# New latents divided by tokens (128, then 192), with the query-latent tiles evicted between the parts

## The reference, cut to what matters

```python
h = rmsnorm(x, lp['norm_mix'])
proj = h @ lp['w_in']                       # pool, q_b, k_b, v_b, q_lat, kv_lat, kr_raw, gates
c_kv = rmsnorm(kv_lat, lp['mla_kv_norm'])   # 256 latents for each of the 320 new tokens
k_rope = apply_rope(kr_raw, pos)
lat_all = jnp.concatenate([past[0], c_kv], axis=1)          # 512 cached tokens come first
kv = (lat_all @ w_kvup).reshape(B, K, MLA_HEADS, MLA_NOPE_DIM + MLA_V_DIM)
k = rmsnorm(jnp.concatenate([k_nope, kr], axis=-1), qk_k_norm)
```

## Time and profile before

| what | value |
|---|---|
| median of 3 runs | 1046.33 us (1045.97 to 1047.3) |
| profiled execution | 1047.23 us |
| its span (first to last instruction) | 1045.3 us |
| granted TensorE clock, mean | 0.998 of full speed |
| PE busy | 1038.8 us (99%) |
| DVE busy | 641.6 us (61%) |
| ACT busy | 506.8 us (48%) |
| POOL busy | 314.3 us (30%) |

### The profile page before, as it was taken

How to read it: one execution, slowest core, us unless ns; L and a number is a source line. 1 busy time by engine, 2 the same in 40 slices (tenths; PEclk the granted TensorE clock), 3 DMA queues, 4 the chain that set the end, 5 groups by cost and what they waited for, 6 DMA issues and landing times.

```text
span 1045.3 us, 20059 instructions
## 1 busy us (share of the span) xinstructions
PE 1038.8 (99%) x7586; PEld 1005.6 (96%) x7586; DVE 641.6 (61%) x1079; ACT 506.8 (48%) x930; POOL 314.3 (30%) x277
## 2 busy tenths in 40 slices
PE   8999999999999999999999999999999999999998
PEld 6899999999999999999998999999999999999998
DVE  6888764445766666543567886554557565565443
ACT  6557755444554444434355585554445444433341
POOL 3365566541221111100133755656312211111000
PEclk9999999999999999999999999999999999999999
DMA  7455533244535544454514544333344354444441
GB/s 243 118 157 124 185 103 120 90 133 142 161 120 164 159 146 155 142 180 145 178 45 137 149 145 135 96 119 122 120 154 152 124 177 141 154 147 146 156 145 67
DMA packets 48707, 146.29 MB, mean 140 GB/s; under 512 B 8800, under 2 KB 14400, under 8 KB 48640
## 3 DMA queue, kind: packets, MB, share of 16 engines
q1 hardware_dynamic: 42416, 143.05, 44.3%
q10 hardware_dynamic: 6224, 2.30, 0.9%
HBM read 142.11 MB, written 3.22 MB: 139 GB/s over the span
## 4 chain that ended last, share of the span: by engine, by line
PE 97%; DVE 2%; DMA 0%; ACT 0%; issue 0%; SPq 0%; ACTq 0%
PE psum L566 29%; PE psum L567 28%; PE psum L568 28%; PE psum L739 1%; PE psum L778 1%; PE psum L761 1%; PE psum L721 1%; PE psum L722 1%; PE psum L726 1%; PE psum L769 1%; PE psum L698 1%; PE psum L811 1%; PE psum L994 0%; PE psum L866 0%; PE psum L693 0%; PE psum L694 0%
## 5 line engine op out<-in xcount | busy, mean ns | idle before, releaser
L566 PE MATMUL psum<-AH,WH 128*128 128x320 f32 x1328 | 414.4, 312 | 0.2
L568 PE MATMUL psum<-AH,WL 128*128 128x320 f32 x1328 | 410.3, 309 | 0.0
L567 PE MATMUL psum<-AL,WH 128*128 128x320 f32 x1328 | 410.2, 309 | 0.0
L566 PEld LDWEIGHTS psum<-AH,WH 128*128 128x128 f32 x1328 | 249.3, 188 | 7.3 <-issue 5.5
L567 PEld LDWEIGHTS psum<-AL,WH 128*128 128x128 f32 x1328 | 249.4, 188 | 0.2
L568 PEld LDWEIGHTS psum<-AH,WL 128*128 128x128 f32 x1328 | 249.3, 188 | 0.0
L1077 ACT CAST WH<-raw 128x1024 fp32r<-128x1024 f32 x166 | 172.7, 1046 | 129.2 <-PE psum L568 127.7
L1515 DVE TENSOR_TENSOR WL<-raw,WH 128x1024 fp32r<-128x1024 f32 x103 | 127.6, 1240 | 114.0 <-ACT WH L1077 113.6
L1978 POOL TENSOR_TENSOR WL<-raw,WH 128x1024 fp32r<-128x1024 f32 x60 | 147.6, 2478 | 114.7 <-ACT WH L1077 95.5
L1709 DVE TENSOR_TENSOR WL<-raw,WH 128x1024 fp32r<-128x1024 f32 x88 | 107.5, 1222 | 49.5 <-ACT WH L1250 48.2
L1983 POOL TENSOR_TENSOR fab<-fa,fb 128x320 f32<-128x320 f32 x44 | 38.6, 878 | 264.6 <-DVE fb L1714 264.6
(11 more groups left out here) (284 smaller groups left out, 1580.1 us busy)
## 6 DMA issues: line engine op xcount, KB each, us to landing
raw<-w_all SPq DMA_DIRECT2D x264, 512.0 KB, 3.5
y_out<-X SPq DMA_DIRECT2D x8, 160.0 KB, 2.7
X<-x_in SPq DMA_DIRECT2D x2, 320.0 KB, 5.7
X<-x_in SPq DMA_DIRECT2D x1, 640.0 KB, 7.4
lat_out<-ckv ACTq DMA_DIRECT2D x2, 320.0 KB, 2.9
scratch<-brel SPq DMA_DIRECT2D x8, 63.8 KB, 4.3
ckv<-lat_in SPq DMA_DIRECT2D x1, 384.0 KB, 5.5
bias<-scratch SPq DMA_DIRECT2D x8, 48.0 KB, 4.5
```

The source lines that it names most:

```text
L566: mm(out, WH[:, slot, c0:c0 + cols], high, start=first, stop=False)
L567: mm(out, WH[:, slot, c0:c0 + cols], low, start=False, stop=False)
L568: return mm(out, WL[:, slot, c0:c0 + cols], high, start=False, stop=last)
```

## The change

The new latents are made in two parts by tokens, 0 to 127 and 128 to 319, each through its own reciprocal, two multiplications, one cast of both chunks and one subtraction. Before, they were made in two parts by chunks of 128 latents. Block 4 of `key_rows` now waits for the first part alone, block 5 for the second. The first query-latent tile is evicted ahead of the first reciprocal, the second behind the first part's multiplications, the third between the second part's reciprocal and its multiplications. `latent_sum` of layer 0 comes behind the second query-latent tile instead of in its middle.

```diff
         def key_rows(l, kb):
-                pe.wait_ge(s.ckv_ready, 3 * l + 3)
-            elif kb != CACHED + 1:
+                pe.wait_ge(s.ckv_ready, 4 * l + 3)
+            elif kb == CACHED + 1:
+                pe.wait_ge(s.ckv_ready, 4 * l + 4)
+            else:
                 pe.wait_ge(s.kn_ready, l * KB + kb - 1)
...
-            dense(l, U_QL + 1, T_QL + 1, between=(lambda: latent_sum(l)) if l == 0 else None)
+            dense(l, U_QL + 1, T_QL + 1)
+            if l == 0:
+                latent_sum(l)
             turn_rope(l, 1)
             dense(l, U_QL + 2, T_QL + 2)
...
             root(l, N_KV, 128, T, 256)
             high(l, U_POOL)
+            act.wait_ge(s.ckv_first, l + 1)
+            nc.scalar.copy(ckvH[:, :, 0:128], ckv[:, :, 0:128]).then_inc(s.ckv_high, 1)
             act.wait_ge(s.stat_applied, l * NNORM + N_KV + 1)
-            nc.scalar.copy(ckvH[:, 0, 0:T], ckv[:, 0, 0:T]).then_inc(s.ckv_high, 1)
-            act.wait_ge(s.ckv_second, l + 1)
-            nc.scalar.copy(ckvH[:, 1, 0:T], ckv[:, 1, 0:T]).then_inc(s.ckv_high, 1)
+            nc.scalar.copy(ckvH[:, :, 128:T], ckv[:, :, 128:T]).then_inc(s.ckv_high, 1)
...
-            r = recip(l, N_KV, 128, T)
-            STT(ckv[:, 0, 0:T], kvr[:, 0, :], col(C_MKV, l), r, ALU.mult, ALU.mult).then_inc(s.stat_applied, 1)
-            STT(ckv[:, 1, 0:T], kvr[:, 1, :], col(C_MKV + 1, l), r, ALU.mult, ALU.mult).then_inc(s.ckv_second, 1)
             scaled(l, T_QL, qlr[:, 0, :])
-            for c in range(2):
-                dve.wait_ge(s.ckv_high, 2 * l + c + 1)
-                ins = TT(ckvL[:, c, 0:T], ckv[:, c, 0:T], ckvH[:, c, 0:T].bitcast(F32), ALU.subtract)
-            ins.then_inc(s.ckv_ready, 1)
-            scaled(l, T_QL + 1, qlr[:, 1, :])
+            dve.wait_ge(s.std_ready, l * NSTAT + N_KV + 2)
+            for n, keys in enumerate((slice(0, 128), slice(128, T))):
+                r = stdk[:, N_KV % 2, keys]
+                link(l, v.reciprocal(r, r))
+                if n == 1:
+                    scaled(l, T_QL + 2, qlr[:, 2, :])
+                for c in range(2):
+                    ins = STT(ckv[:, c, keys], kvr[:, c, keys], col(C_MKV + c, l), r, ALU.mult, ALU.mult)
+                ins.then_inc(s.stat_applied if n else s.ckv_first, 1)
+                if n == 0:
+                    scaled(l, T_QL + 1, qlr[:, 1, :])
+                dve.wait_ge(s.ckv_high, 2 * l + n + 1)
+                TT(ckvL[:, :, keys], ckv[:, :, keys], ckvH[:, :, keys].bitcast(F32), ALU.subtract).then_inc(s.ckv_ready, 1)
             dve.wait_ge(s.both_high, l + 1)
             TT(both[:, :, HALF:128], ckv[:, :, T - HALF:T], both[:, :, 0:HALF].bitcast(F32), ALU.subtract) \
                 .then_inc(s.both_ready, 1)
             low(l, U_POOL)
-            scaled(l, T_QL + 2, qlr[:, 2, :])
```

More of the change, by code:

```diff
@@ L203, in __init__ @@
         self.ckv_high = sem("ckv_high")
-        self.ckv_second = sem("ckv_second")
+        self.ckv_first = sem("ckv_first")
         self.ckv_ready = sem("ckv_ready")
@@ L391, in trunk @@
     raw_ready = [nc.alloc_semaphore(f"raw_ready{i}") for i in range(RING)]
-    DVE_STEPS, POOL_STEPS = 43, 12
+    DVE_STEPS, POOL_STEPS = 44, 12
     def tbank(t):
@@ L672, in key_rows @@
                 pe.wait_ge(s.x_ready, 16 * l + 5)
-                pe.wait_ge(s.ckv_ready, 3 * l + 1)
+                pe.wait_ge(s.ckv_ready, 4 * l + 1)
             elif kb == 1:
                 pe.wait_ge(s.x_ready, 16 * l + 7)
-                pe.wait_ge(s.ckv_ready, 3 * l + 2)
+                pe.wait_ge(s.ckv_ready, 4 * l + 2)
             elif kb == CACHED:
                 pe.wait_ge(s.tile_free, l * NT + T_QL + 2)
-                pe.wait_ge(s.ckv_ready, 3 * l + 3)
-            elif kb != CACHED + 1:
+                pe.wait_ge(s.ckv_ready, 4 * l + 3)
+            elif kb == CACHED + 1:
+                pe.wait_ge(s.ckv_ready, 4 * l + 4)
+            else:
                 pe.wait_ge(s.kn_ready, l * KB + kb - 1)
```

## The result

| | median, us | lowest to highest | ratio to before |
|---|---|---|---|
| before (6 runs beside it) | 1047.02 | 1045.97 to 1047.42 | |
| changed (6 runs) | 1052.62 | 1050.97 to 1055.79 | 1.0061 [1.0051, 1.0072] |

The ratio stands for +6.4 us [5.3, 7.5], the two medians for +5.6. Forecast were +2.6 us (1048.9, range 1047.2 to 1050.3). The sign was right; the loss was mis-sized by more than a factor of two, and the time lies outside the range. The changed kernel also scatters over 4.8 us, the one before over 1.5. The profiled execution of the changed kernel took 1051.97 us, with a span of 1050.2 us.

A forecast was written before the change was run, and what follows sets the result against it. PE, busy 99% of the span, was taken to bound the kernel. Losses of +0.9 us in layer 0 and +1.7 in layer 1 made +2.6 us on the median 1046.33: 1048.9 us, range 1047.2 to 1050.3.

The forecast's parts named there:

- What bounds the kernel: Whole run: PE busy 99% of the span, so only its idle time can be won and every wait is lost.
- The three stalls of layer 0: PE's waits at latent sum, key rows and value rows, 0.40, 0.60 and 0.36 us: 1.36 us to win in all.
- The reciprocals: DVE's reciprocal in two parts: 0.95 us for 128 columns and 1.35 for 192, against 2.15 for 320.
- Rival B: DVE's reciprocal does not shrink with its columns, 2.15 us each part: +2.0 us more, 1050.9 us; chance 0.04.
- The chain behind the second part: Queued work on ACT, DVE and POOL delays block 4's rope rows; PE waits at `turn_keys(4)`, 1.5 to 2.2 us.
- Rival A: PE's wait at `turn_keys(4)` is shorter, down to none: 1045.2 us in full, chance 0.10; half of it 0.24.
- +0.9 and +1.7 us: Forecast losses at `turn_keys(4)`, in layer 0 and layer 1.
- the sum of 2.6: Forecast loss of both layers together, +2.6 us, giving 1048.9 us.
- The failed step: Layer 0, rope rows of block 4: ready at 55.3 by POOL, 55.6 or 55.3 by ACT and DVE; 0.9 us lost.
- Rival C: Lateness goes on to block 5's squares or pool weights, 0.3 to 0.7 us a layer: 1049.5 to 1050.3; chance 0.12.
- That of DMA issues: Skill's rule that DMA initiation time is usually small; with free issues on ACT, 1048.8 instead of 1048.9 us.
- That of a fixed price for each DVE instruction: Skill's rule of fixed latency per DVE instruction reading SBUF: three more a layer, 2 x 0.45 us, 1047.2 us.

The follow-up runs named there:

- the first experiment: Changed kernel with layer 1's third query-latent tile evicted behind the second part's subtraction; 1049.01 us, ratio 1.0028.
- its equal: Changed kernel with the new blocks' small multiply-add written as scalar_tensor_tensor with a second SBUF operand; 1052.75 us, ratio 1.0063.
- both mends: Changed kernel with layer 1's third query-latent tile behind the second part's subtraction and POOL's unit 9 subtraction behind block 4's rope rows; 1047.17 us, ratio 1.0006.

## Why the prediction was half right

*What bounds the kernel.* Right: PE is busy 99% of the span, and each microsecond by which the keys were late is in the time.

*The three stalls of layer 0.* Right: the latent sum and the key rows start without a wait, the second key rows with 0.25 us where 0.4 was forecast.

*The reciprocals.* Right to the digit: 0.95 and 1.35 us, on the line between 8 and 320 columns. Rival B falls.

*The chain behind the second part.* Right in its mechanism: PE waits at `turn_keys(4)` in both layers, released by POOL's rope rows, because the second part comes late (in layer 1 behind the third latent tile, shown by the first experiment) and ACT, DVE and POOL have weights queued ahead of the keys' steps. Rival A falls. In place of +0.9 and +1.7 us, the kernel with the multiply-add on ACT has +0.67 and +1.80: the sum of 2.6 was a good sum of what it contained.

*The failed step: "the squares at 50.28 had the rope rows start 2.95 us later [...] and with the 2.57 us that layer 1 needs [...] 55.3".* Two rows for the same chain differed by 0.38 us, and I took both as bounds instead of asking why. These rows of before, which the prediction had not read, give the reason; first layer 0, then layer 1:

```profile
49.97 2.40 POOL L1978 TENSOR_TENSOR WL<-raw,WH 128x1024 fp32r<-128x1024 f32 x1 [8.26 <-DVE WL L1515]
51.79 0.60 DVE L1555 TENSOR_SCALAR krm<-krm 128x3 f32<-128x3 f32 x1
...
567.11 0.17 DVE L1555 TENSOR_SCALAR krm<-krm 128x3 f32<-128x3 f32 x1
```

In layer 0 of before POOL's subtraction (49.97 + 2.40 = 52.37) overlapped the multiply-add, which ended at 52.39; in layer 1 POOL was done at 566.59. The change moves POOL's start and the squares together, so that the overlap grows from 0.6 us and none to 1.1 us in each layer. The step set POOL's branch and ACT's branch side by side and took the later; in truth the one runs through the other. The multiply-add ends with POOL's subtraction, and root and reciprocal still follow before the rope rows can start: 0.75 us a layer on top of the later branch (0.74 and 0.79 us by the run with the multiply-add on ACT). 2.6 + 2 x 0.75 = 4.1 us, which is what the wait without the fall of the clock costs (3.9 us with the wait filled, 4.0 to 4.4 us in the three executions at full clock).

*The missing term.* I priced a wait of PE at its own length. The profiled execution lost 1.45 us more in layer 1 (4.24 us between the transposes, 2.79 at full clock), because the clock behind the wait was granted at 0.52, and in 12 of 15 executions of this kernel and its equal the mean clock was below 1.0 and the time above all three with 1.0. Filling the wait took that away in five of five executions, with the chain unchanged. Shorter waits had it no more often than the kernel before, whose mean clock was below 1.0 in 6 of 60 executions: with 1.6 us in each layer one of nine, with 1.4 us none of six. Why the fall comes in layer 1 and not in layer 0 with the same wait (with 2.35 us in layer 0 alone it was one execution of eight, which is no more than in the kernel before) stays open.

*Rival C* came about in the form of the clock only: the keys of block 5 were not late (2.79 us behind block 4's at full clock, 2.71 before).

*The range.* Its upper end was the sum plus small lateness. It had no room for a term that multiplies a wait, though the forecast itself put PE's longest wait of that part of the run there.

*The two rules weighed ahead of the run.* That of DMA issues changed nothing, since ACT's order alone left the time the same. That of a fixed price for each DVE instruction was right in size and without effect: DVE's busy time rose by 2.5 us (641.6 to 644.1), 1.5 of them the two longer multiply-adds, which leaves 1.0 us where 2 x 0.45 was forecast; and with both mends layer 1 has all the additional instructions and is as before. A rule that bears on the failed step was not weighed: the Trainium skill ("SBUF — State Buffer", section "SBUF: two separate sides") has DVE and GpSimd share one pair of ports, and calls it "an **exclusive lock**, not a bandwidth split", held for the whole instruction by the one that started first; of DVE's instructions it concerns those in a two-port mode or with two inputs in SBUF. The runs agree: 0.17 us with POOL idle, 0.55 to 1.70 us beside its subtraction, with the end always at POOL's, and the same in the form with two inputs in SBUF. In which mode the other form runs, no trace shows.

## What to carry to other kernels

Where two occurrences of one chain differ in the trace, find the row that differs before either is used as a bound. Read every DVE instruction on the critical chain, the tiny ones above all, against what POOL runs at that moment. Some are held, as both forms of the multiply-add here, and then the price is what is left of POOL's instruction; others are not, as the reductions and the reciprocal here. A long POOL instruction then belongs behind the chain, or the small step on ACT. And a new wait of TensorE of some 2 us is not priced at its length: put work ahead of it, or count with a slow stretch behind it.

## What was not expected of the hardware

- A multiply-add on 128 x 3 elements takes 0.17 us on DVE, and 0.60, 1.14, 1.49 and 1.70 us, by its start, while GpSimd subtracts 128 x 1024 elements (2.4 us); on ScalarE 0.30 us in the same place. A reduction of 96 columns to 3 (0.24 us) and a reciprocal of 8 columns (0.20 us) on DVE beside the same subtraction were not held.
- Behind a wait of 2.3 us the granted clock was 0.52 for 3.3 us in one layer and 1.00 in the other, in the same execution.
- 18 products that nobody reads made the kernel 2.5 us faster than the changed one.
- A reciprocal on DVE took 0.20, 0.95, 1.35 and 2.15 us for 8, 128, 192 and 320 columns, some 6.3 ns for each further column.
